# The recurrence's 64 by 64 products alternate between two row orders in a two-layer RWKV and attention kernel

## The reference, cut to what matters

```python
def _rwkv7_branch(ts, og, mu, w0, w2, a0, a2, k_k, k_a, r_k, gn_g, gn_b, w_o):
...
    k = (k.astype(f32) * (1.0 + (a - 1.0) * k_a.astype(f32))).reshape(hd)
...
    o = _rwkv7_scan(r, decay.reshape(hd), k, v, kk, kk * a)
    o = _layernorm(o, gn_g.reshape(RWKV_HEADS, RWKV_HEAD), gn_b.reshape(RWKV_HEADS, RWKV_HEAD), GN_EPS)
    o = o + jnp.sum(r * k * r_k.astype(f32), axis=-1, keepdims=True) * v
```

## Time and profile before

| | |
|---|---|
| median of 3 runs | 2361.52 us (2360.99 to 2362.99) |
| the profiled execution | 2362.81 us |
| its span | 2361.5 us |
| mean granted TensorE clock | 0.972 |
| PE, DVE, ACT, POOL busy in the span | 94%, 62%, 40%, 20% |
| rounds of the recurrence | from 205.3 us to about 698 us |

### The profile page before, as it was taken

The page is one execution under the profiler, slowest core; times in us unless marked ns, Lnnn a source line. Parts: engine busy times, 40 slices in busy tenths (PEclk is TensorE's granted clock), DMA queues, the critical chain, the costliest instruction groups (busy, mean ns, idle before and its releaser), DMA issues.

```text
span 2361.5 us, 44695 instructions
## 1 busy us (share of the span) xinstructions
PE 2215.4 (94%) x19538; PEld 1947.2 (82%) x19538; DVE 1462.9 (62%) x2338; ACT 938.0 (40%) x1590; POOL 462.2 (20%) x277
## 2 busy tenths in 40 slices
PE   4898999999997999987998999999999999999999
PEld 1677777777766787976888999999988889999987
DVE  3687888888867443496556666633355556777722
ACT  1324434344332434433544444322456655444411
POOL 0344343344310344423231000000000011000000
PEclk7899999999998999997999999999999999999999
DMA  6541011111115324310013223223311013223231
GB/s 237 128 111 55 11 42 42 42 42 42 42 60 173 107 90 126 118 38 10 21 37 112 90 90 91 91 92 94 109 45 37 21 36 115 90 90 90 86 107 67
DMA packets 60290, 184.75 MB, mean 78 GB/s; under 512 B 7200, under 2 KB 11296, under 8 KB 60096
## 3 DMA queue, kind: packets, MB, share of 16 engines
q1 hardware_dynamic: 60096, 181.90, 24.9%
HBM read 174.99 MB, written 6.88 MB: 77 GB/s over the span
## 4 chain that ended last, share of the span: by engine, by line
PE 74%; DVE 16%; ACT 5%; issue 2%; DMA 1%; POOL 0%; SPq 0%; DVEq 0%; ACTq 0%
PE PS L540 59%; PE PS L670 4%; DVE ca L1874 3%; PE PS L1025 2%; PE PS L1152 1%; PE PS L865 1%; PE PS L1120 1%; DVE Swk L2273 1%; DVE mx L2269 1%; DVE kx L1942 1%; PE PS L998 1%; DVE Bf L1948 1%; DMA xt<-in_xT 1%; ACT Lb L1200 1%; DVE acc L1804 1%
## 5 line engine op out<-in xcount | busy, mean ns | idle before, releaser
L2560 POOL TENSOR_TENSOR wlo<-raw,whi 128x1024 fp32r<-128x1024 f32 (+2 forms) x154 | 310.4, 2017 | 926.5 <-ACT whi L1200 921.1
L540 PE MATMUL PS<-nhi,whi 128*128 128x264 f32 x2064 | 440.1, 294 | 12.5 <-DVE nlo L2115 6.9
L540 PE MATMUL PS<-nlo,whi 128*128 128x264 f32 x2064 | 423.1, 287 | 0.0
L540 PE MATMUL PS<-nhi,wlo 128*128 128x264 f32 x2064 | 420.4, 285 | 0.0
L1200 ACT ACTIVATE whi<-raw 128x1024 fp32r<-128x1024 f32 (+3 forms) x322 | 306.4, 953 | 226.4 <-PE PS L540 199.4
L540 PEld LDWEIGHTS PS<-nhi,whi 128*128 128x128 f32 x2064 | 324.0, 191 | 22.1 <-DVE qB L2157 5.6
L540 PEld LDWEIGHTS PS<-nlo,whi 128*128 128x128 f32 x2064 | 324.6, 190 | 0.0
L540 PEld LDWEIGHTS PS<-nhi,wlo 128*128 128x128 f32 x2064 | 324.0, 191 | 0.0
L1786 DVE TENSOR_TENSOR wlo<-raw,whi 128x1024 fp32r<-128x1024 f32 (+1 forms) x168 | 201.1, 1197 | 171.9 <-ACT whi L1200 171.6
L540 PE MATMUL PS<-hhi,whi 128*128 128x512 f32 x648 | 264.5, 408 | 7.4 <-DVE hlo L1853 7.3
L540 PE MATMUL PS<-hhi,wlo 128*128 128x512 f32 x648 | 258.4, 399 | 1.6 <-POOL wlo L2560 1.6
(11 more groups left out here) (351 smaller groups left out, 3533.8 us busy)
## 6 DMA issues: line engine op xcount, KB each, us to landing
raw<-in_wall SPq DMA_DIRECT2D x282, 512.0 KB, 3.6
raw<-in_wall SPq DMA_DIRECT2D x16, 384.0 KB, 3.1
TZ<-g_rows SPq DMA_DIRECT2D x2, 2112.0 KB, 8.4
raw<-in_wall SPq DMA_DIRECT2D x32, 128.0 KB, 2.0
raw<-in_wall SPq DMA_DIRECT2D x16, 256.0 KB, 2.6
g_rows<-gsb SPq DMA_DIRECT2D x8, 328.0 KB
xt<-in_xT SPq DMA_DIRECT2D x1, 2048.0 KB, 13.8
o_rows<-os SPq DMA_DIRECT2D x8, 256.0 KB, 2.2
```

Of the source, the lines that this page charges most:

```text
L540: q = e.matmul(out, cuts[a][:, k * P:(k + 1) * P], (hi_, lo_)[b][:, kr, lo:lo + w], start=start and k == 0 and a == b == 0, stop=stop and ...
L2560: e.tensor_tensor(wlo[slot[i]][:, w], raw[i % NRAW][:, w], whi[slot[i]][:, w].bitcast(F32), ALU.subtract).then_inc(*up("lo_pool", i))
```

## The change

Products of a pair's 64 by 64 blocks are placed in two row orders. In one (that of Tt, Mt, To, XT as stationary operands) block t of half h has its rows where they were for even and odd in a swapped place (`place`); a product goes from one row order to the other, so that for odd t it crosses from partitions 0-63 to 64-127 and back. `crossing` writes these products, what comes from rows 0-63 to one bank and what comes from rows 64-127 to another. W, X, MV and PQ become crossings; XT stays `beside`. A new product, To crossed by the identity, gives XT of level 0. Banks are taken in another way: pairs always take banks 4 and 5, single ones alternate between 2 and 3. The copies read two banks, and the copy of the turned A becomes four.

```diff
+        def place(rows, t, h):
+            return 4 * h + (t ^ (rows.start // 64))
+        def by_bank(ap):
+            return ap.rearrange("p (g r) n -> p r g n", r=2)
+        def crossed_banks(bb):
+            return PS[:, bb[0]:bb[1] + 1, 0:256].rearrange("p r (g n) -> p r g n", n=64)
...
-            def bank(key, *then):
-                b = 2 + turns[0] % 4
-                turns[0] += 1
+            def take(b, key, then):
                 for step in free[b]:
                     on.wait_ge(*at(*step))
-                free[b] = then
+                free[b] = [then]
                 banks[key] = b
                 return b
+            def bank(key, then):
+                turns[0] += 1
+                return take(2 + turns[0] % 2, key, then)
+            def pair_of(key, *then):
+                return [take(4 + r, (*key, r), then[r % len(then)]) for r in range(2)]
...
+                def crossing(bb, lhs, rhs, n=64):
+                    for h in range(2):
+                        for t in range(4):
+                            for half, rows in enumerate(rowsof):
+                                out = rowsof[half ^ (t % 2)]
+                                g, to = place(rows, t, h), place(out, t, h) // 2
+                                q = e.matmul(PS[out, bb[half], to * n:(to + 1) * n], lhs(rows, g), rhs(rows, g),
+                                             start=True, stop=True)
                     return q
...
+                bb = pair_of(("To", j), ("XT", j, 0))
+                crossing(bb, lambda rows, g: eye2[rows, :], lambda rows, g: To[0][rows, g, :]).then_inc(*up("To_crossed", j))
...
-                b = bank(("bonus", j), ("bv", j))
+                b = take(4, ("bonus", j), ("bv", j))
...
-                    b = bank(("W", j, lev), ("W", j, lev))
+                    bb = pair_of(("W", j, lev), ("W", j, lev))
...
-                    beside(b, lambda rows, g: To[lev % 2][rows, g, :], lambda rows, g: X[rows, g, :]).then_inc(*up("W_sum", j, lev))
+                    crossing(bb, lambda rows, g: To[lev % 2][rows, g, :], lambda rows, g: X[rows, g, :]).then_inc(*up("W_sum", j, lev))
...
-                        b = bank(("MV", j), ("MV", j))
+                        bb = pair_of(("MV", j), ("MV", j))
...
-                        b = bank(("X", j, lev), ("X", j, lev))
+                        bb = pair_of(("X", j, lev), ("X", j, lev))
                     b2 = bank(("XT", j, lev), ("XT", j, lev))
                     on.wait_ge(*at("XT", j, lev - 1))
                     on.wait_ge(*at("W", j, lev))
                     if lev < 5:
-                        beside(b, lambda rows, g: XT[rows, g, :], lambda rows, g: Wb[rows, g, :]).then_inc(*up("X_sum", j, lev))
+                        crossing(bb, lambda rows, g: XT[rows, g, :], lambda rows, g: Wb[rows, g, :]).then_inc(*up("X_sum", j, lev))
...
-                bb = [bank(("PQ", j, g), ("PQ" if g == 0 else "PQ_end", j)) for g in range(2)]
+                bb = pair_of(("PQ", j), ("PQ", j), ("PQ_end", j))
...
+                crossing(bb, lambda rows, g: XT[rows, g, :], lambda rows, g: AM[rows, g, :], P).then_inc(*up("PQ_sum", j))
...
+                bb = pair_of(("Rp", j), ("Ph", j))
...
-                act(AM.rearrange("p (h t) n -> p t h n", h=2)[:, :, :, 0:64],
-                    PS[:, banks["A", j], :].rearrange("p (t h n) -> p t h n", t=4, h=2), ACT.Copy).then_inc(*up("Atk", j))
+                for half, rows in enumerate(rowsof):
+                    for r in range(2):
+                        q = act(to[rows, r:4:2, :, 0:64], made_a[rowsof[r], r ^ half:4:2], ACT.Copy)
+                q.then_inc(*up("Atk", j))
...
-                    act(Wb[:, :, :], by8(PS[:, banks["W", j, lev], :]), ACT.Copy).then_inc(*up("W", j, lev))
+                    act(by_bank(Wb), crossed_banks([banks["W", j, lev, r] for r in range(2)]), ACT.Copy).then_inc(*up("W", j, lev))
...
-                on.wait_ge(*at("To_first", j))
-                e.tensor_tensor(XT[:, :, :], eye8, To[0][:, :, :], ALU.subtract).then_inc(*up("XT", j, 0))
                 on.wait_ge(*at("To_turned", j))
                 e.tensor_tensor(X[:, :, :], eye8, by8(PS[:, banks["XT", j], :]), ALU.subtract).then_inc(*up("X", j, 0))
+                on.wait_ge(*at("To_crossed", j))
+                e.tensor_tensor(by_bank(XT), eye2.unsqueeze(1).unsqueeze(1).broadcast_to([P, 2, 4, 64]),
+                                crossed_banks([banks["To", j, r] for r in range(2)]), ALU.subtract).then_inc(*up("XT", j, 0))
```

More of the change, by code:

```diff
@@ L143 @@
     "unit": "unit",
-    "pair_sums": "lora_w lora_a kk_sum square turned bonus MV_sum To_turned W_sum X_sum XT_sum PQ_sum "
+    "pair_sums": "lora_w lora_a kk_sum square turned bonus MV_sum To_turned To_crossed W_sum X_sum XT_sum PQ_sum "
                  "Rp_sum KV_sum O_sum oc_sum gn_sum",
@@ L653, in square @@
                 def square(lhs, out):
-                    bb = [bank((out, j, h), (out, j, h)) for h in range(2)]
+                    bb = pair_of((out, j), (out, j, 0), (out, j, 1))
                     for t in range(4):
@@ L658, in square @@
                             for h in range(2):
-                                o = PS[rowsof[par], bb[h], t * P:(t + 1) * P]
+                                o = PS[rowsof[par], bb[h], (t ^ par) * P:((t ^ par) + 1) * P]
                                 c = 2 * t + par
@@ L664, in square, with beside @@
                                     q.then_inc(*up("square", out, j, h))
-                def beside(b, lhs, rhs, n=64):
-                    for g in range(8 if n == 64 else 4):
+                def beside(b, lhs, rhs):
+                    for g in range(8):
                         for rows in rowsof:
-                            q = e.matmul(PS[rows, b, g * n:(g + 1) * n], lhs(rows, g), rhs(rows, g), start=True, stop=True)
+                            q = e.matmul(PS[rows, b, g * 64:(g + 1) * 64], lhs(rows, g), rhs(rows, g), start=True, stop=True)
+                    return q
+                def crossing(bb, lhs, rhs, n=64):
[6 more added lines that the diff above has]
+                                             start=True, stop=True)
                     return q
@@ L685, in part @@
                 def part(src, k):
-                    return lambda rows, t, h: src[rows, 4 * h + t, 64 * k:64 * k + 64]
+                    return lambda rows, t, h: src[rows, place(rows, t, h), 64 * k:64 * k + 64]
                 def steps_r(src):
-                    return lambda rows, t, h: src[rows, 4 * h + t, 1, :]
+                    return lambda rows, t, h: src[rows, place(rows, t, h), 1, :]
                 on.wait_ge(*at("R", j))
@@ L712, in core @@
                 for lev in range(1, 6):
-                    b = bank(("W", j, lev), ("W", j, lev))
+                    bb = pair_of(("W", j, lev), ("W", j, lev))
                     on.wait_ge(*at("To", j, lev))
                     on.wait_ge(*at("X", j, lev - 1))
-                    beside(b, lambda rows, g: To[lev % 2][rows, g, :], lambda rows, g: X[rows, g, :]).then_inc(*up("W_sum", j, lev))
+                    crossing(bb, lambda rows, g: To[lev % 2][rows, g, :], lambda rows, g: X[rows, g, :]).then_inc(*up("W_sum", j, lev))
                     yield
                     if lev == 1:
-                        b = bank(("MV", j), ("MV", j))
+                        bb = pair_of(("MV", j), ("MV", j))
                         on.wait_ge(*at("Mt", j, 1))
                         on.wait_ge(*at("Vtk", j))
-                        beside(b, lambda rows, g: Mt[rows, g, 0, :],
-                               lambda rows, g: Vtk[rows, g % 4, 64 * (g // 4):64 * (g // 4) + 64]).then_inc(*up("MV_sum", j))
+                        crossing(bb, lambda rows, g: Mt[rows, g, 0, :],
+                                 lambda rows, g: Vtk[rows, g % 4 ^ (rows.start // 64), 64 * (g // 4):64 * (g // 4) + 64]
+                                 ).then_inc(*up("MV_sum", j))
                         yield
@@ L738, in core @@
                     if lev < 5:
-                        beside(b, lambda rows, g: XT[rows, g, :], lambda rows, g: Wb[rows, g, :]).then_inc(*up("X_sum", j, lev))
+                        crossing(bb, lambda rows, g: XT[rows, g, :], lambda rows, g: Wb[rows, g, :]).then_inc(*up("X_sum", j, lev))
                     beside(b2, lambda rows, g: Wb[rows, g, :], lambda rows, g: XT[rows, g, :]).then_inc(*up("XT_sum", j, lev))
                     yield
-                bb = [bank(("PQ", j, g), ("PQ" if g == 0 else "PQ_end", j)) for g in range(2)]
+                bb = pair_of(("PQ", j), ("PQ", j), ("PQ_end", j))
                 on.wait_ge(*at("MV", j))
                 on.wait_ge(*at("XT", j, 5))
-                for g in range(2):
-                    beside(bb[g], lambda rows, k: XT[rows, 4 * g + k, :], lambda rows, k: AM[rows, 4 * g + k, :],
-                           P).then_inc(*up("PQ_sum", j, g))
```

(18 more changed lines are left out.)

## The result

The changed kernel takes 2375.93 us (median of 4 runs, 2375.48 to 2379.02) where the kernel before took 2361.26 beside it (2360.67 to 2362.99): a ratio of 1.0066, interval 1.0054 to 1.0078. It is 14.7 us **slower**, on the predicted side and inside the range, though the forecast of 2371 had about two thirds of the loss.

The account below looks back on a forecast made before the run. It took a braid of PE, ACT and DVE as the bound, with DVE pacing XT5 to the next state step. Terms 10.2 + 1.8 - 2.5 - 0.1 = +9.4 on 2362.8 gave 2372.2, stated as 2371; range 2350 to 2384.

Parts of the forecast that it names:

- What the change removes: PE's work in the eight recurrence rounds: crossings and a shorter PQ save net 5.2 us a round, 41 us at most.
- rival D: Crossings: matmul starts have a 25 ns floor, each of 9 on the path 0.33 us longer, +10, 2381; chance 0.02.
- (1): After W1: XT1 takes w's bank, so X1 waits for s_w and goes at 5.42 us, 1.95 later than before.
- (2): After X1: POOL's To precedes DVE's tap, X2 at 11.4 us against 9.12, XT5 subtracted +0.8 us a round later.
- (3): Before W1: To_crossed on PE's path to the fill costs 0.2 us, or +0.9 a round at half clock.
- (4): Gap before the second state step: clock falls in all rounds, 2 more falls in rounds 1 to 6, +1.8 us.
- (E): Waits at X1 and W3: clock falls a second time, +1 to +2 us a round, up to 2383; part of forecast's 0.54.
- (5): No effect from PQ's saving itself, four AM activations, reads of two banks, or swapped X and XT at level 0.
- Round 7: Last round, without s_w: XT5 2.4 us earlier, PQ 0.95 earlier, To_crossed +0.9, together -2.5 us.
- A: Hold at X1 does not carry on, as s_w ends early or DVE's slack absorbs it: about -8 us, 2354; chance 0.18.
- B: DVE's tap gets in ahead of POOL and the clock falls no more often than now: 0, 2362 us; chance 0.21.
- C: PE sets the pace everywhere and nearly all 41 us saved arrive: 2323 us; chance 0.05.

## Why the prediction was right, and where it fell short

**What the change removes.** The kind of saving was right, its size too large: 29 us off PE's busy time in the trace, against 41 worked out from start distances. The lower clock behind the state step is not what makes the difference: with that gap filled in both kernels it is 29 again (2220.3 to 2191.3, the idle matmuls in both). From W1 to XT5 of round 6, at the full clock in both, PE is busy 21.35 us before and 17.18 after (columns of the windows as above):

```profile
581.09:602.89 21.80, 21.35 (x568) 17.43 (x568) 16.00 (x26) 14.24 (x24) 5.14 (x3) 1.00 0.01 3
...
597.65:620.58 22.93, 17.18 (x568) 12.97 (x568) 16.79 (x25) 14.91 (x24) 4.59 (x4) 1.00 0.01 3
```

That is 4.2 us where the sum had 4.7, and the second falls take some of it back. The sign I had named, some 52 us of PE in a round of 61 to 62, came in round 1, where the clock stays at X1 (52.6 in 62.3), and failed in round 5 (55.10 in 64.43). Groups start 0.51 to 0.52 us behind a crossing of 32 records, 16 ns a record, where I had 0.47. The floor of 25 ns between starts (rival D) does not show. The start times of single records in the traces say how the saving comes about: in `beside` two records, one of each row half, start 7 ns apart and the next two 58 ns behind the first; in a crossing four start 6 to 7 ns apart, and the next four 58 ns behind the first.

**(1) The hold at X1** was named with its place, cause and time: X1 at 5.42 predicted, 5.52 measured, released by s_w; XT1 subtracted at 7.10 predicted, 7.18 measured in the rounds where the clock stays (1, 2 and 6). The run with the banks alone shows the hold without any crossing, and the run with s_w early shows 17.4 us coming back when it goes, part of them by the work that moved with it.

**(2) What is late next** was roughly right. X2 came at 10.93 in rounds 1, 2 and 6, inside my 10.6 to 11.4, and at 11.7 to 12.5 in the other rounds with s_w: in the first three the tap gets in ahead of POOL, and the scan behind it is held instead (2.29 in the timeline of round 5). In the changed kernel one of tap and scan is held in every round with s_w, so which of them it is was not the question that I took it for.

**(3) and (4), To_crossed and the clock**, were right in sum: +8.2 us from Tt to W1, against +9.0 forecast. It is in part luck: round 0 had +0.9 in the sum and lost nothing, while rounds 3 to 7 lost more than their share. The gaps of rounds 2 to 7, 1.9 to 3.3 us before, became 2.2 to 4.2, that of round 1 went from 3.6 to 2.9; the clock fell in every round from 1 to 7, and filling the gap returned 10.2 us of that stretch.

**(E) The second fall** was the upper side of my forecast and came at X1 in four rounds (0, 3, 4 and 5). In rounds 3 to 5 XT1 is subtracted at 8.28 to 8.39 behind W1, not 7.18, 1.1 to 1.2 us later; in round 0 at 7.96. This is the first term that was mis-sized: I had left it out of the sum. Between W1 and XT5 rounds 1, 2 and 6, without a fall at X1, lost 0.3, 0.9 and 1.1 us, 0.8 in the mean as forecast (in round 2 the clock was at 0.50 from 356.6 to 360.0, 14 us behind W1); rounds 3, 4 and 5, with it, lost 1.4, 1.5 and 1.9, and round 0 0.4 where the sum had none. Together that is the 2.7 us over the forecast.

**(5) "Nothing: PQ's saving itself"** is the step that failed. I argued that DVE sets the stretch behind XT5 and so a faster PE changes nothing there. DVE does set it; but a faster PE sets POOL off earlier, and POOL's wlo then gets in ahead of a tap that it used to follow. That cost 0.55 to 0.8 us in each of rounds 1 to 4; with what rounds 5 and 6 gained the line comes to +2.3 where I had -0.9, all of it round 0's, and round 0 gained nothing. The wait was in my list under W and X, and I did not carry it to PQ. The four activations for AM took 1.54 us together and stayed hidden, as said.

**Round 7** gained 1.5 us between W1 and XT5 instead of 2.4; in its last level PE's records stand apart by 1.06 us with "issue" as the only reason the trace gives. The gap is no part of the change: in the six other runs with crossings this stretch, with the same steps, takes 16.84 to 17.19 us. Without the 1.06 the gain is 2.6, near the forecast. What made the gap stays open.

**The rivals.** A is what the kernel does once s_w is early, as the prediction put it (it decides at s_w's end): X1 at 2.82, and a time of 2358.5 where A had 2354. B was right that the tap gets in ahead of POOL, but needed a clock that falls no more often; it fell more often. C was far off: with PE at 92% the chain lost PE and gained DVE, as argued from the earlier trace rows.

The Trainium skill (TensorEngine Tiling (Array Packing), Gotcha 1: PSUM Pressure) says that tiling adds pressure on PSUM, with different row tiles writing to different banks. The change follows that, and the run with the banks alone puts a number on the pressure here: 29 us, more than the crossings bring in the given order. Where the page goes on that different row tiles cannot access one bank at the same time, the trace does not agree: in `beside` the records of the two row halves start 7 ns apart and write one bank, in different partitions. No run here puts two row tiles of a crossing into one bank.

What stays open: what decides whether the clock falls behind a short wait (see below), and whether MV in the unused halves of banks 4 and 5 would shorten the chain further, which wasn't tried.

## What to carry to other kernels

A faster engine is worth nothing, or less, if what it needs for its speed (here two banks at a time out of four) is held by a step off its chain; list who frees each bank in the new order before counting the gain, and move the holder first. Ask also what the faster engine sets off sooner: here a POOL operation got in ahead of DVE's. And where an engine waits in the same place in every round, look at the clock behind that place: two matmuls that nobody reads gained 6 to 12 us in four kernels.

## What the runs showed of the hardware that I had not expected

- The granted clock fell behind a wait of 2.10 us at X1 in rounds 3, 4 and 5 and did not in rounds 1, 2 and 6 with the same wait. With the gap ahead of the state step filled, rounds 1 to 6 take the same 13.98 us from Tt to W1 at the full clock and wait the same 2.10 us, and it fell in rounds 1 and 5 and not in 2, 3, 4 and 6. With 1.54 us at XT1 in place of it, it fell there in no round. But with s_w early it was at 0.50 from 534.38 to 536.38, behind a wait of only 1.35 us for W3 (531.80). So the length of the last wait does not decide by itself; what else does, these runs don't show.
- DVE's tap reads two SBUF tensors and took 2.90 us beside POOL's 2.40 us of wlo, 0.74 without: it stands still while POOL works. The Trainium skill (GPSIMD Engine Reference, Specifications) lists the SBUF interfaces as shared with VectorE, with contention for operations with two SBUF inputs; the trace agrees. The subtractions of XT with one operand in PSUM kept their 0.69 beside POOL.
- Filling a gap cost next to nothing where the gap was long enough: the two idle matmuls take 1.98 us of PE a round, in time that PE spent waiting, and the stretch around them became shorter. Only in round 7 of the kernel before, with a gap of 1.87 us, did it get longer, by 0.35.
